# A float32r decoder layer whose four split-weight slots are laid 32 bytes further apart

## What is computed

```
x += 1/2 * (silu(n(x) @ w_gate) * (n(x) @ w_up)) @ w_down          # d_ff = 5632
h  = n(x) @ w_in                                                   # split into 12 parts
x += concat(HGRN2 gated recurrence, native sparse attention) @ w_out
x += cross attention over 256 memory tokens (4 heads of 128)
x += 1/2 * (silu(n(x) @ w_gate2) * (n(x) @ w_up2)) @ w_down2
out = n(x)                                                         # n is RMSNorm
```

## Time and profile before

| | us |
|---|---|
| median of 2 runs | 2152.25 |
| lowest, highest | 2150.37, 2154.13 |
| the profiled execution's own time | 2151.12 |
| its span (first to last instruction) | 2149.2 |
| TensorE busy | 2088.2 (97%) |
| VectorE busy | 1117.6 (52%) |
| ScalarE busy | 940.5 (44%) |
| mean granted TensorE clock, share of full | 0.977 |

### The profile page before, as it was taken

The page is one execution under the profiler, slowest core; times in us unless marked ns, Lnnn a source line. Parts: engine busy times, 40 slices in busy tenths (PEclk is TensorE's granted clock), DMA queues, the critical chain, the costliest instruction groups (busy, mean ns, idle before and its releaser), DMA issues.

```text
span 2149.2 us, 25561 instructions
## 1 busy us (share of the span) xinstructions
PE 2088.2 (97%) x9679; PEld 1728.5 (80%) x9679; DVE 1117.6 (52%) x1400; ACT 940.5 (44%) x1181; POOL 0.2 (0%) x4
## 2 busy tenths in 40 slices
PE   6999999999999999999999999899999999999997
PEld 5788888888888888878888987678888888888886
DVE  5545454454544445676567555454544545444444
ACT  6544444444444445454453244444444444433442
POOL 0000000000000000000000000000000000000000
PEclk9999999999999999999997699899999999999999
DMA  6566666666565655665540055266666666755553
GB/s 224 176 196 186 193 187 187 190 190 188 186 191 179 191 186 176 195 219 158 152 147 1 18 184 178 72 175 189 186 191 188 191 190 185 209 187 189 187 189 124
DMA packets 194343, 372.23 MB, mean 173 GB/s; under 512 B 12904, under 2 KB 15456, under 8 KB 194144
## 3 DMA queue, kind: packets, MB, share of 16 engines
q1 hardware_dynamic: 190176, 366.62, 56.5%
q10 hardware_dynamic: 4096, 4.64, 0.6%
HBM read 369.11 MB, written 2.10 MB: 173 GB/s over the span
## 4 chain that ended last, share of the span: by engine, by line
PE 94%; DVE 2%; ACT 2%; ACTq 1%; issue 1%; DVEq 0%
PE psum L1202 87%; PE psum L1213 2%; PE psum L1484 1%; PE psum L1438 1%; PE psum L1306 1%; PE psum L1406 0%; PE psum L1419 0%; ACT w_hi L422 0%; DVE xT_lo L780 0%; ACT xT_hi L445 0%; ACT silu_gate L452 0%; PE psum L1570 0%; DVE att L1089 0%; DVE w_lo L744 0%; ACTq L475 0%
## 5 line engine op out<-in xcount | busy, mean ns | idle before, releaser
L744 DVE TENSOR_TENSOR w_lo<-w_raw,w_hi 128x1024 fp32r<-128x1024 f32 x696 | 850.5, 1225 | 920.3 <-ACT w_hi L422 919.1
L422 ACT ACTIVATE w_hi<-w_raw 128x1024 fp32r<-128x1024 f32 x696 | 736.5, 1060 | 1041.5 <-PE psum L1202 1028.9
L1202 PE MATMUL psum<-w_hi,xT_hi 128*128 128x512 f32 (+1 forms) x1824 | 712.6, 391 | 7.7 <-DVE xT_lo L780 4.9
L1202 PE MATMUL psum<-w_hi,xT_lo 128*128 128x512 f32 (+1 forms) x1824 | 708.0, 388 | 0.0
L1202 PE MATMUL psum<-w_lo,xT_hi 128*128 128x512 f32 (+1 forms) x1824 | 707.9, 388 | 0.0
L1202 PEld LDWEIGHTS psum<-w_hi,xT_hi 128*128 128x128 f32 x1824 | 342.8, 188 | 80.1 <-DVE xT_lo L780 6.2
L1202 PEld LDWEIGHTS psum<-w_hi,xT_lo 128*128 128x128 f32 x1824 | 342.8, 188 | 70.4
L1202 PEld LDWEIGHTS psum<-w_lo,xT_hi 128*128 128x128 f32 x1824 | 342.9, 188 | 68.6
L1202 PE MATMUL psum<-w_hi,ffT_hi 128*128 128x512 f32 x928 | 369.4, 398 | 2.4 <-DVE ffT_lo L1169 2.4
L1202 PE MATMUL psum<-w_hi,ffT_lo 128*128 128x512 f32 x928 | 367.3, 396 | 0.0
L1202 PE MATMUL psum<-w_lo,ffT_hi 128*128 128x512 f32 x928 | 367.1, 396 | 0.0
(11 more groups left out here) (199 smaller groups left out, 709.0 us busy)
## 6 DMA issues: line engine op xcount, KB each, us to landing
w_raw<-in_g SPq DMA_DIRECT2D x176, 512.0 KB, 3.6
w_raw<-in_u SPq DMA_DIRECT2D x176, 512.0 KB, 3.7
w_raw<-in_d SPq DMA_DIRECT2D x176, 512.0 KB, 4.2
w_raw<-in_w_in SPq DMA_DIRECT2D x88, 512.0 KB, 3.6
w_raw<-in_w_out SPq DMA_DIRECT2D x32, 512.0 KB, 3.6
w_raw<-in_wk SPq DMA_DIRECT2D x8, 512.0 KB, 4.7
w_raw<-in_wv SPq DMA_DIRECT2D x8, 512.0 KB, 4.0
w_raw<-in_cw SPq DMA_DIRECT2D x8, 512.0 KB, 3.8
```

Of the source, the lines that this page charges most:

```text
L422: nc.scalar.activation(w_hi[:, slot], w_raw[:, slot], ACT.Copy).then_inc(w_hi_ready, 1)
L744: nc.vector.tensor_tensor(w_lo[:, slot], w_raw[:, slot], w_hi[:, slot].bitcast(F32), ALU.subtract)\
L1202: mm = nc.tensor.matmul(dst[:, t, 0:width], act_t, w[:, slot, kk, 0:width], start=(first and kk == 0 and n == 0), stop=(last and kk == KT_ ...
```

## The change

A constant `PAD = 8` (elements) is added. `w_hi` and `w_lo` are no longer placed as four packed slots but each as one flat row of 4 * (1024 + 8) + 32 = 4160 elements, of which a view picks slots that begin 1032 elements (4128 bytes) apart. Each slot's 1024 elements stay contiguous. The view has the old shape [partition, slot, 2, 512], so that no other line changes.

```
+PAD = 8
...
-        w_hi = put("w_hi", [P, SLOTS, KT_U, NW], F32R)
-        w_lo = put("w_lo", [P, SLOTS, KT_U, NW], F32R)
+        w_hi, w_lo = (put(n, [P, SLOTS * (KT_U * NW + PAD) + PAD * SLOTS], F32R)[:, 0:SLOTS * (KT_U * NW + PAD)]
+                      .rearrange("p (s x) -> p s x", s=SLOTS)[:, :, 0:KT_U * NW]
+                      .rearrange("p s (k n) -> p s k n", k=KT_U) for n in ("w_hi", "w_lo"))
```

## The result

The changed kernel took 2174.7 us, the median of two runs (2169.2 and 2180.2), against 2152.25 before: the ratio is 1.0106, with a 95% interval of 1.0073 to 1.014. So it is slower, by less than 2% but clearly more than the runs of one kernel differ. Timed again in four runs beside seven of the kernel before, it took 2182.7 us against 2151.2, a ratio of 1.0147 [1.0131, 1.0164], that is +31.5 us.

A forecast was written before the change was run, and what follows sets the result against it. The prediction took TensorE's 8256 matmuls, a count times a pace, to bound the kernel. It added 0 us to 2151.1 us and, with the median of the runs 1.1 us above, forecast 2152 us, range 2130 to 2184.

The forecast's parts named there:

- rival (a): xT stages: the new slots break the even beat, 5.7 ns on 5472 matmuls, +31 us, 2183 us; chance 0.20.
- The bound, the count, the pace: TensorE sets the beat: 5472 xT matmuls at 226.7 ns and 2784 ffT matmuls at 232.4 ns, together 8256.
- No cost on ScalarE, VectorE, DMA and SyncE's queue: Slot writes and loads: nothing taken, 40 to 70 ns either way per instruction as bound, covered by 5.9 us of slack.
- TensorE's reads, 0 ns: Matmuls reading the moved slots: 0 ns change likeliest, the only term without cover; 1 ns each would be 8.3 us.
- Rival (b): ffT stages: ffT gets the even beat, -5.7 ns on 2784 matmuls, -16 us, 2136 us; chance 0.10.
- Rival (c): All matmuls: excess over 213.3 ns is a weight-load clash of like slots; all gone 2026 us, half 2089; chance 0.12.
- (d): Matmuls on slots 1 and 3, off a 64-byte multiple, cost extra: 240 ns each, +47 us, 2199 us; chance 0.08.
- (e): Coarse memory regions, not low bits, make the 5.7 ns, so no time change; included in the 0.50 for no change.
- The Trainium skill's rule: TensorE's slot reads: two read ports of its own, never waits on anyone, so the sum is 0.
- What a measurement can tell: Whole kernel: about 2% (43 us) can be told from no change; 0.83 given to a result within 2%.
- What would show it: Profile after: pieces of 43.5 and 61.35 us if right; 44.6 or 59.8 us, shorter pieces or uneven gaps otherwise.
- The period of four units: Timeline after: gaps differing from unit to unit with a period of four units would show that low bits matter.

The follow-up runs named there:

- the second profile: Profile of the unaltered changed kernel's second timing, beside the kernel before; span 2180.6 us, timing 2182.7 us against 2151.2.
- the sweep: TensorE alone, no layer, 49 blocks of 48 matmuls with other start addresses: 226.7 to 227.3 ns at multiples of 256 bytes, 229 to 238 ns otherwise.
- the bare kernel: TensorE alone, no layer, blocks of 48 matmuls; with units at 0, 32, 64, 96 bytes as in the changed kernel, 11.09 and 11.13 us.

## Why the prediction was wrong

The forecast was no change, and the kernel is slower by 31.5 us (22 by its first two runs). The measured times lie in the range only because the range reached to rival (a). Point by point:

- *The bound, the count, the pace*: right. The kernel is 8256 matmuls at a pace, at full clock, and the 5.7 ns between the paces was the thing to explain.
- *No cost on ScalarE, VectorE, DMA and SyncE's queue*: right, 1061 and 1225 ns as before.
- *TensorE's reads, 0 ns*: wrong, and this is the step that failed. I took it from line 1306: 229.6 ns with stationary slices at all sorts of low addresses, hence "low bits in themselves do little there". That row couldn't say so. Its slices have 66 columns, and with 64 columns each of the three distances that were tried costs 230 to 231 ns (L78 to L80). So the row most likely showed a loss already taken; 66 columns themselves were not run. What the runs showed in place of the 0 ns: +5.3 ns for each matmul with an `xT` slice (226.7 to 232.0) and +0.9 with an `ffT` slice (232.4 to 233.3). The second support, that no `ffT` slice was slower than another, was no evidence either: the slices are 512 bytes apart, so all had the same distance modulo 256.
- *Rival (a)*, with 0.20: right in place and mechanism, and near in price: 5.7 x 5472 = +31 us, 2183 us, against 2182.7 measured. That the two agree so closely is luck: it had 5.7 ns where 5.3 came, and left out 0.9 ns on `ffT`, and by chance the mix of four distances costs gate and up (232.0 ns) about as much as its single distance cost `ffT` (232.4).
- *Rival (b)*: its mechanism is the same, and its reason against was right: `ffT` stood at 128, and 128 + 0, 32, 64, 96 never comes to 0 modulo 256. The gain that it priced at 16 us is there for a change that sets the distance: 14.4 us.
- *Rival (c)*, a clash that a spread removes: wrong. The equal low bits were the good case. An excess of at least 13.4 ns stays at every distance.
- *Rivals (d) and (e)*: wrong. Slots off the 64-byte grid cost next to nothing of themselves (227.3 ns, L87), and the far region is as quick as the near one.
- *The Trainium skill's rule* (SBUF — State Buffer, "Who interferes with whom", two read ports, TensorE waits on no one): no other engine slows TensorE, which agrees: the pace is 226.7 ns in the layer and with TensorE alone (L51). But with TensorE alone, the pace still hangs on where its own two reads start, 226.7 against 229 to 238 ns, so the rule doesn't give a sum of 0 here.
- *What a measurement can tell*: the forecast put it at 2% (43 us). The runs told +31.5 and -14.4 us from no change, with intervals about 3 us to either side.
- *What would show it*: 44.6 us for a piece is what came (44.54), and TensorE's wait for `w_lo` stayed small (0.3 us in the second profile). The period of four units didn't come. Every twelfth start of the changed kernel's timeline, so one line for each unit, shows two:

```profile
320.68 0.40 PE L1204 MATMUL psum<-w_hi,xT_hi 128*128 128x512 f32 x1
...
323.49 0.40 PE L1204 MATMUL psum<-w_hi,xT_hi 128*128 128x512 f32 x1
...
326.24 0.40 PE L1204 MATMUL psum<-w_hi,xT_hi 128*128 128x512 f32 x1
...
329.05 0.39 PE L1204 MATMUL psum<-w_hi,xT_hi 128*128 128x512 f32 x1
...
331.81 0.40 PE L1204 MATMUL psum<-w_hi,xT_hi 128*128 128x512 f32 x1
```

The units take 2.81, 2.75, 2.81 and 2.76 us, where before each took 2.72. The two slow ones fit the distances 32 and 96, which cost the same (L55, L58 of the sweep). The two others fit 64 and 0, and the unit at 0 doesn't come down to 2.72, as in the bare kernel.

What I should have weighed more: the timeline already showed two beats for one shape, the even one where both operands stood at equal low addresses and the uneven one where they stood 128 bytes apart. That was the only pair of rows with the very shape in question, and it spoke for (a).

## What to carry to other kernels

Where a kernel is bound by a stream of float32r matmuls (128 columns stationary, 512 moving), lay the tensors out so that moving and stationary slices start at the same address modulo 256 bytes: in the down stages here it was worth 5.6 ns of 232 per matmul. A padding between slots is free if it is a multiple of that (256 bytes, 2148.8 us) and cost 31.5 us at 32 bytes. Other shapes need a sweep of their own. Take the price of an operation from rows of its own shape: a row of another shape may have no good case to lose.

## What the runs showed of the hardware

- The spacing of back-to-back float32r matmuls of 128 by 128 by 512 is 226.7 to 227.3 ns when the two slices start a multiple of 256 bytes apart, 229.0 to 234.6 ns at the other multiples of 16 bytes and 227.9 to 238.5 ns at the steps between, with TensorE alone and at a granted clock of 1.00. In bfloat16 it is 215.8 to 216.3 ns at all five distances tried.
- A unit of 12 such matmuls at distance 0 takes 2.72 us behind another at distance 0, and 2.76 behind one at 96 bytes.
- With 96 stationary columns the quiet distance is another: 226.7 ns at 128 bytes, 230.0 at 0. With 64 and 32 columns none of the three distances tried was below 230.
- VectorE's and ScalarE's instructions took 1225 and 1061 ns for 1024 elements as before (medians), with slots 32, 64 and 96 bytes later.
- In the attention stretch the granted clock can come back early in one run and not in the next (last third 1.00 against 0.58), which is worth 14 us: more than many a change.
